# Attention kernel: the last 32 keys of each four rows are scaled into a buffer of their own and turned as one operand

## The reference, cut to what matters

```python
def neighbourhood_attention(q, k, v, rpb):          # 2048 tokens = 32 rows of 64; 8 heads of 64
    ...
    s = jnp.einsum('bhrcd,bhrjkd->bhrcjk', qg, kg).astype(jnp.float32) + bias[None]
    s = jnp.where(col_mask[:, None, :], s, -jnp.inf)
    p = jax.nn.softmax(s.reshape(B, NA_HEADS, rows, GRID_W, kh * GRID_W), axis=-1).reshape(s.shape)
    o = jnp.einsum('bhrcjk,bhrjkd->bhrcd', p, vg)
    return o.transpose(0, 2, 3, 1, 4).reshape(B, T, NA_W)
```

## Time and profile before

| what | value |
| --- | --- |
| time, median of 3 runs | 1991.86 us (1990.2 to 1992.28) |
| the profiled execution, its own time | 1991.98 us |
| its span, first to last instruction | 1989.6 us |
| TensorE busy | 1934.0 us, 97% of the span |
| VectorE, ScalarE, GpSimd busy | 50%, 32%, 28% |
| granted TensorE clock, mean | 0.989 of full |

### The profile page before, as it was taken

How to read it: one execution, slowest core, us unless ns; L and a number is a source line. 1 busy time by engine, 2 the same in 40 slices (tenths; PEclk the granted TensorE clock), 3 DMA queues, 4 the chain that set the end, 5 groups by cost and what they waited for, 6 DMA issues and landing times.

```text
span 1989.6 us, 27490 instructions
## 1 busy us (share of the span) xinstructions
PE 1934.0 (97%) x10489; PEld 1553.8 (78%) x10489; DVE 986.3 (50%) x2099; ACT 631.7 (32%) x1316; POOL 557.5 (28%) x839
## 2 busy tenths in 40 slices
PE   6999999989999899999999999999998999799998
PEld 5888878768888788888887788888885666588887
DVE  6564555674756433115776111223215666576765
ACT  5421212132444432102222102121115555555552
POOL 3122324122552222100101001222215545444442
PEclk8999999999999999999999999999999999899999
DMA  5232324245886755312221125765636565856763
GB/s 174 80 105 74 99 83 114 88 146 202 278 284 201 255 180 159 106 48 90 70 74 65 45 61 157 216 191 174 208 126 178 144 182 180 284 165 235 247 224 112
DMA packets 240574, 303.59 MB, mean 153 GB/s; under 512 B 41526, under 2 KB 164310, under 8 KB 240412
## 3 DMA queue, kind: packets, MB, share of 16 engines
q1 hardware_dynamic: 213004, 215.84, 35.7%
q0 software_dynamic: 25136, 81.81, 11.3%
q10 hardware_dynamic: 2304, 4.20, 0.6%
HBM read 194.71 MB, written 107.54 MB: 152 GB/s over the span
## 4 chain that ended last, share of the span: by engine, by line
PE 89%; DVE 3%; DMA 3%; issue 2%; ACT 1%; POOL 1%; SPq 0%; POOLq 0%; ACTq 0%; DVEq 0%
PE banks L145 24%; PE banks L147 24%; PE banks L146 24%; PE banks L1851 3%; PE banks L1830 3%; PE banks L1811 2%; PE banks L1832 2%; PE banks L2407 2%; PE banks L2409 1%; PE banks L2142 1%; PE banks L2377 1%; DMA iraw<-hT 1%; PE banks L231 1%; DVE sa L486 0%; DMA iraw<-in_w_in 0%
## 5 line engine op out<-in xcount | busy, mean ns | idle before, releaser
L145 PE MATMUL banks<-hT,wu 128*128 128x512 f32 x512 | 202.2, 395 | 1.5 <-DVE hT L217 1.5
L147 PE MATMUL banks<-hT,wu 128*128 128x512 f32 x512 | 200.4, 391 | 0.0
L146 PE MATMUL banks<-hT,wu 128*128 128x512 f32 x512 | 200.2, 391 | 0.0
L145 PE MATMUL banks<-iT,wub 128*128 128x512 f32 x384 | 151.3, 394 | 1.9 <-DVE wub L1258 1.9
L145 PE MATMUL banks<-iT,wua 128*128 128x512 f32 x384 | 150.9, 393 | 2.3 <-DVE iT L1258 2.3
L145 PE MATMUL banks<-wub,iT 128*128 128x512 f32 x384 | 150.5, 392 | 0.0
L147 PE MATMUL banks<-iT,wub 128*128 128x512 f32 x384 | 149.7, 390 | 0.0
L147 PE MATMUL banks<-iT,wua 128*128 128x512 f32 x384 | 149.5, 389 | 0.0
L146 PE MATMUL banks<-wub,iT 128*128 128x512 f32 x384 | 149.5, 389 | 0.0
L146 PE MATMUL banks<-iT,wua 128*128 128x512 f32 x384 | 149.5, 389 | 0.0
L147 PE MATMUL banks<-wub,iT 128*128 128x512 f32 x384 | 149.4, 389 | 0.0
(11 more groups left out here) (282 smaller groups left out, 4171.0 us busy)
## 6 DMA issues: line engine op xcount, KB each, us to landing
iraw<-in_w_in SPq DMA_DIRECT2D x36, 512.0 KB, 4.3
wa<-in_w_ada SPq DMA_DIRECT2D x48, 256.0 KB
raw<-in_pool_in_w SPq DMA_DIRECT2D x16, 512.0 KB, 4.4
yT<-sg POOLq DMA_DIRECT2D x32, 256.0 KB, 2.9
oraw<-yT SPq DMA_DIRECT2D x32, 256.0 KB, 4.6
xr<-in_x SPq DMA_DIRECT2D x16, 512.0 KB, 4.3
h<-h POOLq DMA_DIRECT2D x16, 512.0 KB, 3.8
hT<-tr POOLq DMA_DIRECT2D x16, 512.0 KB, 5.4
```

The source lines that it names most:

```text
L145: e.matmul(ps, lh, rh, start=first, stop=False)
L146: e.matmul(ps, lh, rl, start=False, stop=False)
L147: return e.matmul(ps, ll, rh, start=False, stop=last)
```

## The change

GpSimd's scaling of one head's probabilities becomes two instructions: the first 128 columns of each block are scaled in place as before, and the last 32 columns of each block are scaled into a new buffer `er`, one block next to the other (96 or 64 columns in all). TensorE turns that buffer with one transpose of 128 x 96 or 128 x 64 in place of three or two matmuls of 128 x 32. The result lies where it lay. `scaled` now counts two for each head, and the waits on it are changed to match.

```diff
@@ class Attention, __init__
         self.pr = [k.at(f"p{i}", 96 + 1.875 * i, [P, 480]) for i in range(8)]
+        self.er = [k.at(f"e{i}", 57.5 + 0.375 * i, [P, 96]) for i in range(8)]
@@ def pool
                 w.wait_ge(*self.inverse.ge(q + 1))
                 w.wait_ge(*self.blocked.last())
+                nb = self.blocks(q)
                 for n in (2 * q, 2 * q + 1):
-                    e.tensor_scalar(self.pr[n % 8][:, 0:N], self.pr[n % 8][:, 0:N], self.st[:, n, 2:3], 1.0, ALU.mult, ALU.mult).then_inc(*self.scaled.inc())
+
+                    rows = self.pr[n % 8][:, 0:N].rearrange("p (b c) -> p b c", b=nb)
+                    e.tensor_scalar(rows[:, :, 0:P], rows[:, :, 0:P], self.st[:, n, 2:3], 1.0, ALU.mult, ALU.mult).then_inc(*self.scaled.inc())
+                    e.tensor_scalar(self.er[n % 8][:, 0:32 * nb].rearrange("p (b c) -> p b c", b=nb), rows[:, :, P:160], self.st[:, n, 2:3], 1.0,
+                                    ALU.mult, ALU.mult).then_inc(*self.scaled.inc())
@@ def pe
-                    w.wait_ge(*self.scaled.ge(n + 1))
+                    w.wait_ge(*self.scaled.ge(2 * n + 2))
                     if q >= 1:
                         w.wait_ge(*(self.pt_act if x else self.pt_dve).ge(q))
                     for j in range(nb):
                         e.transpose(self.pT[x][:, j * P:(j + 1) * P], probs[:, 160 * j:160 * j + P], self.ident[:])
-                    for j in range(nb):
-                        t = e.matmul(self.pT[x][32 * j:32 * j + 32, nb * P:(nb + 1) * P], probs[:, 160 * j + P:160 * (j + 1)], self.ident[:],
-                                     start=True, stop=True)
-                    t.then_inc(*self.pt_full.inc())
+                    e.transpose(self.pT[x][0:32 * nb, nb * P:(nb + 1) * P], self.er[n % 8][:, 0:32 * nb], self.ident[:]).then_inc(*self.pt_full.inc())
@@ class Tail, def sp
-        w.wait_ge(*att.scaled.ge(128))
+        w.wait_ge(*att.scaled.ge(256))
```

## The result

The changed kernel takes 1962.0 us in the median (1959.8 to 1963.1, four runs), beside 1992.1 us before; the ratio is 0.9846, with a 95% interval of 0.9829 to 0.9863. That is 30 us less; 1960 was forecast, in a range of 1950 to 1975. The profiled execution took 1959.8 us, its span is 1957.5 us, 32.1 less than before.

What follows compares the result with a forecast made beforehand. TensorE's pace times 64 steps was taken to bound the attention stage. Saving 40 us on turns, less 6 at tables, 1 for masks and additions, 0.5 each at start and end, gave -32: 1960 us, range 1950 to 1975.

Steps and rivals of the forecast that it cites:

- TensorE's saving: Turns in attention: one run of transposes replaces four groups, saving 0.63 us in 48 pairs, 0.61 in 16, 40 us.
- upper bound of 0.36: New 96- or 64-column transpose: at most the replaced small-matmul group's 0.36 us, 32 us more for all 128; 0.11 taken.
- The sum: Whole kernel: -40 + 6 + 1 + 0.5 + 0.5 = -32 us, from 1991.98 to 1960.0.
- The reason given: TensorE's turns: time lies in changes between operand kinds more than in work; three changes inside one pair's turns.
- GpSimd's price: Scaling on GpSimd: 0.58 + 0.34 us a head, a pair 1.84 where it was 1.31; covered by 0.7 in ordinary steps.
- The tables: Where GpSimd builds the next table: it ends at 17.9 us, TensorE wants 15.9; 2 us late three times, 6 given back.
- Masks, start and end: Attention's masks in step 22 and additions in steps 60 and 61: 1 us together; start 0.5, end 0.5.
- The start's own term: First turns of attention: they wait for GpSimd, with two heads' second scaling instructions on that way, 0.5 us added.
- VectorE's wait: Sign in attention: VectorE's wait for the values' product falls from 72 to about 35 us.
- rival E: TensorE in attention: the clock falls to half as transposes replace matmuls, steps up to 5.8 us, about 2110; 2%.
- What I read from the earlier trace: Early transposes: the clock rose to full behind transposes alone, against the skill's rule that it does not engage for them.
- The loads: Queues in attention's heaviest stretch: share rises from 0.86 to 0.95, under the 1.06 reached elsewhere.

Runs made afterwards that it cites:

- the reordering: The kernel before, with both heads' transposes issued first, then both heads' small matmuls: 1976.3 us, ratio 0.9924.
- the undone turn: The changed kernel with the new buffer turned by two or three 32-column matmuls again, GpSimd still scaling in two instructions: 1992.5 us, ratio to before 1.0000.
- the first and third placements: Changed kernel, GpSimd's table building moved: quarters in odd steps 9 to 15, 1959.4 us; odd steps 7 to 15, memsets in three parts, masks and additions moved, 1953.3 us.

## Why the prediction was right, point by point

**TensorE's saving** was forecast as 0.63 and 0.61 us a pair, 40 in all. Measured: turns of 1.03 and 0.81 for 1.65 and 1.41, steps of 2.90 for the 2.91 forecast, 38.8 over 62 distances. The transpose of 96 or 64 columns cost the 0.11 of the nearest row, and its upper bound of 0.36 was far off.

**The sum** was -32 and the medians differ by 30.1. It held in part because its errors cancel. The saving was 1.2 us smaller than put, and 8.8 us were given back where 8 stood, so the stage between its first and last-but-one products is 30.0 us shorter. The profiled execution's 32.1 comes nearer to the forecast only by the 1.95 us of its start, which go with its clock.

**The reason given,** that the time is in the changes between two kinds of operand more than in the work, is shown for the changes: they are 0.28 us of the 0.62 by the reordering alone, and the third is some 0.12 more (0.34 less 0.22 of work). The rest is work. My reading of a change's price from the order of time was a little low: the reordered kernel's turns took 1.37 us where I put 1.41, since I had the second head's small matmuls at 0.25 and they add 0.22. The Trainium skill (TensorEngine Tiling (Array Packing), Key Properties) says that changing the tiling mode drains the engine. The 0.14 us for each change agree with that, though no run shows whether they are a drain; its part on narrow operands did not bite, since the 64-column transpose between full ones started 0.11 us behind its neighbour.

**GpSimd's price** was 0.58 + 0.34 us a head; the rows say 0.581 and 0.340. That it is free in ordinary steps is shown by the undone turn for the old step and by 2.90 us for the new one. The sum for a pair was 0.1 us too high, since the instructions start 0.02 us closer than they last.

**The tables:** 2 us late each, 6 in all, was forecast; 2.1 and 6.3 were measured. Two small errors cancel in it: GpSimd's round took 13.4 us (1567.57 to 1581.01) where I put 13.7, and TensorE wanted its end 0.2 earlier, since the scores in front of it are the short ones, 0.64 us and not 0.86. Moving the work away removed nearly all of it at the first two tables and nothing at the third, where the transfers take its place.

**Masks, start and end** were put at 2 us together. The masks of step 22 gave back 0.3. The additions of steps 60 and 61 with the end gave back 1.8, more than the 1.2 that was left for them; 0.8 of it went when the additions were moved, and the rest was not tried. The start's own term can't be told from the clock: the first products with the values came 1.95 us earlier, in an execution whose clock rose 2.2 us earlier (at 1503.4 and not 1505.6 us). The 0.5 us at the start of the fourth head pair (from the products at 1643.98 to those at 1647.28, 3.30 us for 2.83) was not forecast. GpSimd stood idle for 1.27 us in front of a store there, though its data was ready, and the scaling behind it was late. The same step is long in every variant of the changed kernel (by 0.15 where the mid steps are 3.12 us); why the store began late was not tried.

**VectorE's wait** for the value products was to fall from 72 to about 35 us and fell to 52. I had taken off the whole 0.6 us of every step; but in the kernel before 14.4 us of VectorE's idle time stood in front of its copy, waiting for the turns, and 5.1 us stands there now. That is 9 us of the difference; the rest is about as large as the 8.8 us in which TensorE was late, and VectorE may have waited with it, which is not shown. Nothing in the sum hangs on it.

**The clock** stayed at full from 1503.4 to 1688 us, with transposes in place of the small matmuls; rival E did not come. Its price, about 2110, does not come out of its own terms, which give 1992 + 371 - 218 = 2145; nothing rests on it. What I read from the earlier trace rows against the rule of the Trainium skill (TensorE: Matmul & The Clock Gate, Part 4) holds in some executions only. These are the eight transposes behind the first sixteen, with nothing but transposes before them, in two executions of the changed kernel:

```profile
13.21 1.10 PE L231 MATMUL banks<-ident,xe 128*128 128x128 f32 x8 [2.40 <-DVE xe L212]
12.78 1.97 PE L231 MATMUL banks<-ident,xe 128*128 128x128 f32 x8 [1.88 <-DVE xe L212]
```

The first has the full pace, (1.10 - 0.27) / 7 = 0.12 us, the second half of it, (1.97 - 0.48) / 7 = 0.21. Of the eleven executions profiled, two are like the first, six like the second, and three change from full to half within the eight. So the clock stood at full behind transposes alone in five executions, and in six it did not. The clock's column reads 1.00 in both cases, so only the pace tells the level there.

**The loads** were judged right for this kernel (no wait of the scores for a load) and wrong as to the room. I put the share at 0.95, under what the queues can do. It is 0.87 at the first table (1565 to 1590 us), but 1.00 in the changed kernel itself from 1610 to 1620 us, ahead of the third, and in the first and third placements the keys came late there.

## What to carry to other kernels

Look at the starts of small TensorE instructions, not at their durations: where a group of another kind starts later than the pace inside a run, bring the operands into one form, or at least into one order (0.14 us for each change here). Before the engine that bounds is made faster, write the next engine's round down for every step, those with odd jobs above all, and put such jobs in pieces behind its part of the round. When one lateness is gone, look for the one that it covered: here the transfers' at the third table.

## What was not expected of the hardware

Reordering the same instructions gained 16 of the 30 us that the change gains (0.28 us a pair). Consecutive scalings on GpSimd start 0.02 us closer than their durations. Where the clock rises at the start of attention moves from one execution to the next (between 1503 and 1510.5 us of the span in those profiled), and with it the first distance between value products, 2.85 us in one execution of the changed kernel, 3.54 in another and 5.07 in two of the other placements: as much as one table.
